# A two-layer transformer in one kernel: other work between a layer's end and the first products of the next

## The chip, the cores and the metric

The kernel runs on one core of one Trainium2 chip. The metric is the device time of one execution in microseconds (us). The kernel before was timed three times; the median is 2736.37 us.

## What is computed

512 tokens of 2048 features go through two layers of a hybrid attention block and then a third block (a pooling mixer, a state-space mixer and a gated embedding). In float32 throughout. Cut to what matters here:

```python
def rms_norm(x, w, eps=NORM_EPS):
    xf = x * lax.rsqrt(jnp.mean(x * x, axis=-1, keepdims=True) + eps)
    return xf * w

def hybrid_layer(x, ...):
    h = rms_norm(x, pre_w)
    proj = h @ w_in                      # 2048 -> 5952, split into q, k, v, gates, latents c_q, c_kv ...
    qc = rms_norm(c_q, q_norm_w) @ w_uq  # latent of 512
    kvc = rms_norm(c_kv, kv_norm_w) @ w_ukv
    y = ...                              # three kinds of attention, gated
    out = y @ w_out
    return x + rms_norm(out, post_w)     # "new x"
```

The layer runs twice. The second block begins in the same way: norm of x, then `h @ w_in_2`.

## The kernel before

**Layout.** Everything is kept feature-major: a matrix of 512 tokens by 2048 features is 16 tiles of 128 partitions (features) by 512 (tokens), called kt = 0 to 15. A float32 product is made of three matmuls (`product`, lines 1792 to 1794): high part of the weights by high part of the activations, high weights by low activations, low weights by high activations. So for every weight tile ScalarE makes the high part (`w_hi`, line 560) and GpSimd the low one (`w_lo`, line 547), and for every activation tile ScalarE makes `act_hi` and VectorE `act_lo` (line 1006, `lo_part`). Weights come in units of 512 KB through a ring of four slots (unit u lies in slot u mod 4): the DMA queue of SyncE refills a slot when the low part of its unit is made; ScalarE splits a unit into a slot when TensorE is done with the unit four before it (`split_one`).

**What sets the order.** There is no scheduler. Each engine has its own program, written out by hand, and the engines wait for each other by semaphores. ScalarE's program carries the weight splits as calls of `split_until` and `through`, placed between its other work, and all of it runs strictly in that order.

**From one layer to the next.** At the end of layer l, after the last product with `w_out`, all of this follows (it happens twice: the first handoff goes to layer 1, the second to the third block):
- `ones_product` sums squares over the partitions on TensorE, `root` takes the square root on ScalarE, `rms` the reciprocal on VectorE (lines 1864, 588, 1027). The result `rstd` stands in SBUF.
- A loop over the 16 tiles on VectorE: tile times `rstd` (line 1425), times the weight and plus the old x (line 1426, the old x stands in `wide`), then the low part of the tile before (line 1006), and one addition to the running sum of squares (line 1435).
- The same loop on ScalarE: high part (line 782), square (line 784); after tiles 7, 11 and 15 some weight units are split, after tiles 7 and 15 half of x is stored to DRAM (line 788, semaphore `x_out`).
- TensorE runs `first_pairs`: for each tile kt four output tiles (two in `gemm_ps`, two in `s_ps`), 12 matmuls, each tile after its low part is there. In front of each group of four tiles it waits for the two weight units of the group.

**Behind it.** TensorE goes on with `ckr` (in layer 1 four units of 12 matmuls; after two of them `ones_product` of the new x), then `ckv`, whose results go to `gemm_ps` again, so VectorE must have taken the first results out of it (line 998, `take`). VectorE takes them times `rstd` of the new x, into tiles 12 to 15, and only after the stores of x have landed, because they read those tiles. Then it sums their squares (`square_sum`), for a `ones_product` that comes after three of the four `ckv` units of 24 matmuls.

The very first products, of the input x, go through `first_pairs` as well, with tiles split by `split_x0` (line 689) and `lo_part`.

## Time and profile before

| | |
|---|---|
| median of three runs | 2736.37 us (2735.83 to 2737.54) |
| the profiled execution | 2740.65 us, span of its profile 2738.9 us |
| TensorE matmul | busy 2653.3 us (97% of the span), 12650 matmuls |
| VectorE | 1455.6 us (53%) |
| GpSimd | 1181.3 us (43%) |
| ScalarE | 939.1 us (34%) |
| mean granted TensorE clock | 0.99 |

TensorE leaves some 86 us of the span free, and all other engines are far from full. The table of instructions by line says what each costs; the list of waits says for whom TensorE stood still; the timeline of an engine shows single instructions, with the idle time in front of them and what ended it. A matmul row's length includes its way through the array: in a busy stretch the next one starts well before the row ends.

### The profile page before, as it was taken

What the parts mean: (1) busy time and instruction counts of PE and PEld (TensorE: products, weight loads), DVE (VectorE), ACT (ScalarE), POOL (GpSimd) and SP (SyncE); (2) the same over time, 40 slices, a digit from 0 to 9 for tenths busy, and PEclk for the clock granted to TensorE, in tenths of its full rate; (3) what the DMA queues carried; (4) which work ended last, traced back from release to release, by engine and by line L of the source; (5) the groups of instructions that cost most, each with busy time, mean ns of one, the idle gap of its engine ahead of it and who ended that gap; (6) DMA issues with size and microseconds to landing.
All of it is one profiled execution on the core that took longest, in us unless ns stands there. A gap on an engine that the chain in (4) does not pass through costs nothing. (4 is left out here: it accounts for less than half of the span.)

```text
span 2738.9 us, 34832 instructions
## 1 busy us (share of the span) xinstructions
PE 2653.3 (97%) x12650; PEld 2110.3 (77%) x12650; DVE 1455.6 (53%) x1962; ACT 939.1 (34%) x1898; POOL 1181.3 (43%) x860
## 2 busy tenths in 40 slices
PE   8999999999999899999999999989999999999997
PEld 6877877877788678787777778868777688788885
DVE  6453137449622835312654973286799996300524
ACT  5233214225422423321431552241455443322321
POOL 6542443442354345244344234535333356455552
PEclk9999999999999999999999999999999999999998
DMA  5332332221433243233223143224322233433332
GB/s 180 101 112 63 100 85 69 77 85 47 161 92 100 78 130 115 70 92 92 62 77 88 51 149 105 93 106 137 96 78 85 93 123 108 155 96 96 106 93 77
DMA packets 246202, 268.74 MB, mean 98 GB/s; under 512 B 20544, under 2 KB 237248, under 8 KB 243648
## 3 DMA queue, kind: packets, MB, share of 16 engines
q1 hardware_dynamic: 240512, 222.33, 27.4%
q10 hardware_dynamic: 5568, 44.74, 4.1%
q8 instruction: 82, 1.34, 0.2%
q14 instruction: 40, 0.33, 0.0%
HBM read 246.06 MB, written 20.97 MB: 97 GB/s over the span
## 5 line engine op out<-in xcount | busy, mean ns | idle before, releaser
L547 POOL TENSOR_TENSOR w_lo<-w_raw,w_hi 128x512 fp32r<-128x512 f32 x856 | 1181.1, 1403 | 1516.2 <-ACT w_hi L560 1516.0
L1792 PE MATMUL gemm_ps<-act_hi,w_hi 128*128 128x512 f32 x2720 | 1086.0, 399 | 48.2 <-DVE act_lo L1006 36.9
L1794 PE MATMUL gemm_ps<-act_hi,w_lo 128*128 128x512 f32 x2720 | 1063.2, 391 | 0.0
L1793 PE MATMUL gemm_ps<-act_lo,w_hi 128*128 128x512 f32 x2720 | 1062.8, 391 | 0.0
L560 ACT CAST w_hi<-w_raw 128x512 fp32r<-128x512 f32 x856 | 486.5, 618 | 1321.5 <-PE gemm_ps L1794 1105.5
L1792 PEld LDWEIGHTS gemm_ps<-act_hi,w_hi 128*128 128x128 f32 x2720 | 512.5, 188 | 188.3 <-issue 55.3
L1794 PEld LDWEIGHTS gemm_ps<-act_hi,w_lo 128*128 128x128 f32 x2720 | 512.5, 188 | 109.1
L1793 PEld LDWEIGHTS gemm_ps<-act_lo,w_hi 128*128 128x128 f32 x2720 | 513.1, 189 | 105.8 <-issue 4.3
L998 DVE TENSOR_TENSOR tiles<-gemm_ps,rstd 128x512 f32<-128x512 f32 (+1 forms) x50 | 33.9, 689 | 262.3 <-PE gemm_ps L1794 258.5
L1405 DVE COPY tiles<-gemm_ps 128x512 f32 x28 | 19.4, 692 | 179.0 <-PE gemm_ps L1794 178.6
L1737 DVE TENSOR_TENSOR tiles<-gemm_ps,att 128x512 f32<-128x512 f32 x16 | 11.0, 690 | 141.6 <-PE gemm_ps L1794 141.6
L1792 PE MATMUL to_ps<-act_hi,w_hi 128*128 128x512 f32 x192 | 75.9, 395 | 0.0
L1072 DVE TENSOR_TENSOR att<-to_ps,sin_t 128x512 f32<-128x512 f32 x40 | 27.5, 689 | 88.9 <-PE to_ps L1893 88.8
L1794 PE MATMUL to_ps<-act_hi,w_lo 128*128 128x512 f32 x192 | 74.7, 389 | 0.0
L1793 PE MATMUL to_ps<-act_lo,w_hi 128*128 128x512 f32 x192 | 74.7, 389 | 0.0
L1110 DVE TENSOR_REDUCE small<-s_ps 128x1 f32<-128x128 f32 (+5 forms) x48 | 26.7, 557 | 81.4 <-PE s_ps L1937 81.0
L1952 PE MATMUL to_ps<-cst,att 128*128 128x128 f32 x384 | 59.1, 278 | 7.0 <-ACT att L638 4.6
L616 ACT ACTIVATE att<-att,small 128x256 f32<-128x256 f32 (+1 forms) x128 | 60.1, 473 | 15.1 <-DVE small L1106 14.2
L1952 PEld LDWEIGHTS to_ps<-cst,att 128*128 128x128 f32 x384 | 47.7, 142 | 18.4 <-issue 5.5
L1767 DVE SCALAR_TENSOR_TENSOR att<-att 128x512 f32 x14 | 11.3, 807 | 90.0 <-ACT att L971 90.0
L1083 DVE TENSOR_TENSOR tiles<-tiles,att 128x512 f32<-128x512 f32 x36 | 56.1, 1560 | 1.2
L623 ACT ACTIVATE att<-s_ps,small 128x128 f32<-128x128 f32 (+1 forms) x64 | 31.8, 500 | 71.0 <-DVE small L1111 71.0
(396 smaller groups left out, 3158.1 us busy)
## 6 DMA issues: line engine op xcount, KB each, us to landing
w_raw<-in_w_in_dram SPq DMA_DIRECT2D x248, 512.0 KB
w_raw<-in_w_out_dram SPq DMA_DIRECT2D x96, 512.0 KB
w_raw<-in_w_ple_gate_dram SPq DMA_DIRECT2D x32, 512.0 KB
gate_scratch<-att ACTq DMA_DIRECT2D x16, 512.0 KB, 2.7
x_scratch<-tiles ACTq DMA_DIRECT2D x4, 2048.0 KB, 8.4
att<-x_scratch ACTq DMA_DIRECT2D x2, 4096.0 KB, 12.6
w_raw<-in_w_glu_dram SPq DMA_DIRECT2D x32, 256.0 KB
tiles<-in_x_dram ACTq DMA_DIRECT2D x4, 1024.0 KB, 8.0
```

Of the source, the lines that this page charges most:

```text
L547: ins = pool.tensor_tensor(w_lo[:, s, k], w_raw[:, s, k], w_hi[:, s, k].bitcast(F32), ALU.subtract)
L560: act.copy(w_hi[:, slot, k:k + 2], w_raw[:, slot, k:k + 2]).then_inc(whi_done, 1)
L616: act.activation(v, v, ACT.Exp, bias=sm[:, 4 + j:5 + j], scale=SCALE[br], accum_out=sm[:, 8 + j:9 + j])
L623: last = act.activation(prob[n % 3][:, c * 512:c * 512 + nk], src, ACT.Exp, bias=sm[:, 4 + c:5 + c], scale=SCALE[br], accum_out=sm[:, 8 + ...
L998: tt(dst, ps[:, f, :], scale[:], ALU.mult).then_inc(bank_taken[f], 1)
L1072: tt(sq[:, n % 2], t_ps[:, n % 2, :], sin_t[:], ALU.mult).then_inc(rope_read, 1)
L1083: tt(t, t, sq[:, n % 2], ALU.add).then_inc(roped, 1)
L1110: own.link(dve.reduce_max(sm[:, 0:nc_], src, AX))
L1792: pe.matmul(ps, left_hi, right_hi, start=first, stop=False, skip_group_check=True)
L1793: pe.matmul(ps, left_hi, right_lo, start=False, stop=False, skip_group_check=True)
L1794: return pe.matmul(ps, left_lo, right_hi, start=False, stop=last, skip_group_check=True)
L1952: mm = pe.transpose(t_ps[:, a, k * 128:(k + 1) * 128], prob[n % 3][:, a * 512 + k * 128:a * 512 + (k + 1) * 128], ident)
```

## The change

- The reciprocal of the handoff is written to PSUM (`o_ps[:, 0]`), and tile times reciprocal to `o_ps[:, 1]`; both were in SBUF. Before each such product VectorE now waits until the multiply-add of the tile before is done with `o_ps[:, 1]`.
- Of the 15 additions of squares in the loop, 6 stay; the rest is done after the loop in wider additions, and tiles 14 and 15 go to a second input of `ones_product` (one more matmul, at layer 1 and the third block).
- `first_pairs` waits for the high part of a tile, does the eight matmuls with it, then waits for the low part and does the other four.
- The results of the first products are copied out by ScalarE as they are, to tiles 4 to 7 (`raw_out`), and VectorE multiplies them by `rstd` there later (`scale_raw`).
- x is stored in three parts (tiles 0 to 7, 8 to 11, 12 to 15), with a semaphore each.

The core of the diff (left out: the semaphores of the store, the same waits in the third block):

```diff
@@ -670,6 +671,13 @@
 
+            def raw_out(key, first, pairs_out):
+
+                for r in range(pairs_out):
+                    for f in range(2):
+                        act.wait_ge(mm_done, unit_end(key, 6 + r) + f + 1)
+                        act.copy(tiles[:, first + 2 * r + f], (gemm_ps, s_ps)[r][:, f, :]).then_inc(bank_taken[f], 1)
+
             n_par = 0
@@ -707,6 +715,7 @@
             through(("cq", 0), 8)
+            raw_out(("cq", 0), 4, 2)
 
@@ -715,7 +724,7 @@
                         act.wait_ge(mm_done, unit_end(("ukv", l - 1), 4))
-                    act.copy(sub_hi[:, kt], tiles[:, 12 + kt]).then_inc(lat_hi, 1)
+                    act.copy(sub_hi[:, kt], tiles[:, 4 + kt]).then_inc(lat_hi, 1)
                 through(("uq", l), 4)
@@ -783,13 +793,18 @@
                     if kt % 4 == 3 and kt > 4:
-                        split_until(at[("cq", 1) if l == 0 else ("si", 0)][0] + {7: 6, 11: 8, 15: 12 if l else 14}[kt])
-                    if kt % 8 == 7:
-                        act.dma_start(x_dram[:, kt - 7:kt + 1, :], tiles[:, kt - 7:kt + 1, :]).then_inc(x_out, 16)
+                        split_until(at[("cq", 1) if l == 0 else ("si", 0)][0] + {7: 6, 11: 8, 15: 12}[kt])
+                    if kt in (7, 11, 15):
+                        part = slice(0 if kt == 7 else kt - 3, kt + 1)
+                        act.dma_start(x_dram[:, part, :], tiles[:, part, :]).then_inc(x_out[kt // 4 - 1], 16)
                 if l == LAYERS - 1:
-                    act.wait_ge(sq_sum, 15 * l + 13)
+                    act.wait_ge(sq_sum, 6 * l + 6)
                     act.dma_start(att[:, SSM_AT:SSM_AT + SSM_COLS],
                                   ssm_params[:, POLE_COLS:POLE_COLS + SSM_COLS]).then_inc(ssm_in, 16)
+                if l == 0:
+                    act.wait_ge(x_out[0], 16)
+                    raw_out(("cq", 1), 4, 2)
+                    split_until(at[("cq", 1)][0] + 14)
                 root(f"x{l + 1}")
@@ -1020,12 +1035,18 @@
 
-            def rms(norm):
+            def rms(norm, dst=None):
 
                 to = rstd_lat if norm[0] == "c" else rstd[:]
                 dve.wait_ge(sqrt_done, NORMS[norm] + 1)
-                dve.reciprocal(to, to).then_inc(rstd_done, 1)
+                dve.reciprocal(to if dst is None else dst, to).then_inc(rstd_done, 1)
                 dve.wait_ge(rstd_done, NORMS[norm] + 1)
+
+            def scale_raw(first, count):
+
+                for k in range(first, first + count):
+                    mark = own.mark(tt(tiles[:, k], tiles[:, k], rstd[:], ALU.mult))
+                own.wait(mark)
 
@@ -1266,14 +1287,12 @@
                     rms(f"x{l}")
-                    dve.wait_ge(x_out, 32 * l)
-                for r in range(2):
-                    for f in range(2):
-                        round_done(("cq", l), 6 + r, f)
-                        take(f, tiles[:, 12 + 2 * r + f], ps=s_ps if r else gemm_ps)
-                dve.wait_ge(bank_taken[0], at[("cq", l)][1] + 3)
-                dve.wait_ge(bank_taken[1], at[("cq", l)][1] + 3)
-                square_sum(12)
+                    for s in x_out[:2]:
+                        dve.wait_ge(s, 16 * l)
+                for b in bank_taken:
+                    dve.wait_ge(b, at[("cq", l)][1] + 3)
+                scale_raw(4, 4)
+                square_sum(4)
                 dve.nop().then_inc(bank_taken[0], 1)
@@ -1283,12 +1302,14 @@
                         rms(f"cq{l}")
-                        latent(l, 0, 12, "qn")
+                        latent(l, 0, 4, "qn")
                         dve.wait_ge(rcol_tp, l + 1)
                         dve.tensor_copy(C("rcol", 0, 4), t_ps[:, 0, :].rearrange("p (t n) -> p t n", t=4)[:, :, 0])\
                             .then_inc(rcol_done, 1)
 
                 dve.wait_ge(lat_ready, 8 * l + 4)
+                if l:
+                    dve.wait_ge(x_out[2], 16 * l)
                 for r, (u, dst) in enumerate(((0, 12), (1, 14), (None, 9))):
@@ -1415,25 +1436,32 @@
                     dve.tensor_copy(tiles[:, 14 + f], gemm_ps[:, f, :]).then_inc(bank_taken[f], 1)
-                rms(f"post{l}")
+                rms(f"post{l}", o_ps[:, 0, :])
                 dve.wait_ge(x_back, 16 * (l + 1))
                 pre = [C("pre", 16 + kt) if l == 0 else C("gain2", kt) for kt in range(KT)]
                 for kt in range(KT + 2):
                     if kt < KT:
                         if kt >= 14:
                             dve.wait_ge(bank_taken[kt % 2], at[("wo", l)][1] + 9)
-                        own.link(tt(tiles[:, kt], tiles[:, kt], rstd[:], ALU.mult))
-                        stt(tiles[:, kt], tiles[:, kt], C("post", 16 * l + kt), wide[:, kt],
+                        if kt:
+                            dve.wait_ge(xnew, KT * l + kt)
+                        own.link(tt(o_ps[:, 1, :], tiles[:, kt], o_ps[:, 0, :], ALU.mult))
+                        stt(tiles[:, kt], o_ps[:, 1, :], C("post", 16 * l + kt), wide[:, kt],
                             ALU.mult, ALU.add).then_inc(xnew, 1)
                     if 1 <= kt <= KT:
                         dve.wait_ge(xnew, KT * l + kt)
                         lo_part(f"x{l + 1}", kt - 1, pre[kt - 1])
-                    if kt > 2:
+                    if 10 <= kt < 16:
                         dve.wait_ge(sq_done, KT * (l + 1) + kt - 1)
-                        if kt > 3:
-                            dve.wait_ge(sq_sum, 15 * l + kt - 3)
-                        tt(wide[:, 0], wide[:, 0], wide[:, kt - 2], ALU.add).then_inc(sq_sum, 1)
-                dve.wait_ge(sq_sum, 15 * (l + 1))
+                        if kt > 10:
+                            dve.wait_ge(sq_sum, 6 * l + kt - 10)
+                        tt(wide[:, 7], wide[:, 7], wide[:, kt - 2], ALU.add).then_inc(sq_sum, 1)
+                dve.wait_ge(sq_sum, 6 * (l + 1))
+                own.link(tt(wide_flat[:, 0:4 * T], wide_flat[:, 0:4 * T], wide_flat[:, 4 * T:8 * T], ALU.add))
+                own.link(tt(wide_flat[:, 0:2 * T], wide_flat[:, 0:2 * T], wide_flat[:, 2 * T:4 * T], ALU.add))
+                own.mark(tt(wide[:, 0], wide[:, 0], wide[:, 1], ALU.add))
+                dve.wait_ge(sq_done, KT * (l + 2))
+                own.link(tt(wide[:, 14], wide[:, 14], wide[:, 15], ALU.add))
                 dve.nop().then_inc(ssq_in, 1)
@@ -1856,10 +1886,10 @@
 
-            def ones_product(norm, squares=(sq[:, 0],), lasts=0):
+            def ones_product(norm, squares=(sq[:, 0],), lasts=None):
                 pe.wait_ge(ssq_in, SSQ[norm])
                 for i, s in enumerate(squares):
-                    if i:
+                    if i and lasts is not None:
                         pe.wait_ge(last_sq, lasts + i)
@@ -1872,16 +1902,21 @@
                         pe.wait_ge(bank_taken[1], r0 + 1)
+                    groups = [(p, f, slice(128 * f, 128 * f + 128)) for p in range(2) for f in range(2)]
                     for k in range(UK):
-                        ready_tiles(version, 4 * j + k + 1)
-                        for p, ps in enumerate((gemm_ps, s_ps)):
-                            slot = (2 * j + p) % RING
-                            for f in range(2):
-                                w = slice(128 * f, 128 * f + 128)
-                                mm = product(ps[:, f, :], w_hi[:, slot, k, w], w_lo[:, slot, k, w], act_hi[:, 4 * j + k],
-                                             act_lo[:, 4 * j + k], j == 0 and k == 0, j == 3 and k == 3)
-                                if k == UK - 1:
-                                    mm.then_inc(mm_done, 1)
+                        first, last, kt = j == 0 and k == 0, j == 3 and k == 3, 4 * j + k
+                        pe.wait_ge(hi_done, VERS[version] + kt + 1)
+                        for p, f, w in groups:
+                            ps, slot = (gemm_ps, s_ps)[p][:, f, :], (2 * j + p) % RING
+                            pe.matmul(ps, w_hi[:, slot, k, w], act_hi[:, kt], start=first, stop=False, skip_group_check=True)
+                            pe.matmul(ps, w_lo[:, slot, k, w], act_hi[:, kt], start=False, stop=False, skip_group_check=True)
+                        ready_tiles(version, kt + 1)
+                        for p, f, w in groups:
+                            ps, slot = (gemm_ps, s_ps)[p][:, f, :], (2 * j + p) % RING
+                            mm = pe.matmul(ps, w_hi[:, slot, k, w], act_lo[:, kt], start=False, stop=last,
+                                           skip_group_check=True)
+                            if k == UK - 1:
+                                mm.then_inc(mm_done, 1)
 
@@ -2008,7 +2043,7 @@
                     if j == 1:
-                        ones_product(f"x{l}", [wide[:, 0]])
+                        ones_product(f"x{l}", [wide[:, 0], wide[:, 14]] if l else [wide[:, 0]])
                 u0, first_free = at[("ckv", l)][0], at[("cq", l)][1] + 1
```

Three places in the engines' order. First VectorE in the first handoff, around tiles 4 to 6 (`tiles` is x, `col` the norm weights, `att` the old x or the squares, `to_ps` holds `o_ps`). Before:

```order
L1425 TENSOR_TENSOR tiles<-tiles,rstd 128x512
L1426 SCALAR_TENSOR_TENSOR tiles<-tiles,col,att 128x512 [waits dve_own]
L1006 SCALAR_TENSOR_TENSOR act_lo<-tiles,col,act_hi 128x512 [waits hi_done,xnew]
L1435 TENSOR_TENSOR att<-att 128x512 [waits sq_sum,sq_done]
L1425 TENSOR_TENSOR tiles<-tiles,rstd 128x512
```

and changed:

```order
L1448 TENSOR_TENSOR to_ps<-tiles,to_ps 128x512 [waits xnew]
L1449 SCALAR_TENSOR_TENSOR tiles<-to_ps,col,att 128x512 [waits dve_own]
L1021 SCALAR_TENSOR_TENSOR act_lo<-tiles,col,act_hi 128x512 [waits hi_done,xnew]
L1448 TENSOR_TENSOR to_ps<-tiles,to_ps 128x512 [waits xnew]
L1449 SCALAR_TENSOR_TENSOR tiles<-to_ps,col,att 128x512 [waits dve_own]
```

The addition is gone from these tiles, and the product has a wait of its own.

Then VectorE behind the last tile of that handoff, changed:

```order
L1021 SCALAR_TENSOR_TENSOR act_lo<-tiles,col,act_hi 128x512 [waits hi_done,xnew]
L1460 TENSOR_TENSOR att<-att 128x2048 [waits sq_sum]
L1461 TENSOR_TENSOR att<-att 128x1024 [waits dve_own]
L1462 TENSOR_TENSOR att<-att 128x512 [waits dve_own]
L1464 TENSOR_TENSOR att<-att 128x512 [waits sq_done]
L1042 RECIPROCAL rstd<-rstd 128x512 [waits dve_own,sqrt_done]
L1048 TENSOR_TENSOR tiles<-tiles,rstd 128x512 [waits bank0_taken,x_out1,bank1_taken,x_out0,rstd_done]
```

Four wider additions stand behind the last low part where two of 512 stood, and the first read of the new `rstd` no longer reads a bank that TensorE waits for.

Last ScalarE behind tile 15 of the first handoff, changed (the casts are splits of weight units):

```order
L561 CAST w_hi<-w_raw 128x512 [waits mm_done,raw_in3]
L561 CAST w_hi<-w_raw 128x512
L799 DMA x_scratch<-tiles 128x2048
L679 COPY tiles<-gemm_ps 128x512 [waits mm_done,x_out0]
L679 COPY tiles<-gemm_ps 128x512 [waits mm_done]
L679 COPY tiles<-s_ps 128x512 [waits mm_done] x2
L561 CAST w_hi<-w_raw 128x512 [waits mm_done,raw_in0]
```

Before, four more casts stood ahead of the store, and no copy; now the store comes first, then the copies, then those four casts, and only then the root.

## Rows read from the trace of the kernel before

**Rows 1.** TensorE's waits in the whole span: us in total, times, longest

```profile
PE gemm_ps L1792 <- DVE act_lo L1006: 36.9, 13, 12.8
```

**Rows 2.** Timelines at the start: first matmul, first low part, second weight unit

```profile
12.77 0.76 PE L1792 MATMUL gemm_ps<-act_hi,w_hi 128*128 128x512 f32 x1 [12.77 <-DVE act_lo L1006]
...
10.76 1.87 DVE L1006 SCALAR_TENSOR_TENSOR act_lo<-tiles,col,act_hi 128x512 fp32r<-128x512 f32 x1 [9.42 <-ACT act_hi L689]
...
10.81 1.27 POOL L547 TENSOR_TENSOR w_lo<-w_raw,w_hi 128x512 fp32r<-128x512 f32 x1
```

**Rows 3.** Timelines of the first handoff: first high part on ScalarE, then TensorE

```profile
897.77 0.72 ACT L782 ACTIVATE act_hi<-tiles,col 128x512 fp32r<-128x512 f32 x1 [4.93 <-DVE tiles L1426]
...
899.93 0.76 PE L1792 MATMUL gemm_ps<-act_hi,w_hi 128*128 128x512 f32 x1 [7.82 <-DVE act_lo L1006]
905.91 0.39 PE L1794 MATMUL gemm_ps<-act_hi,w_lo 128*128 128x512 f32 x1
908.22 0.39 PE L1792 MATMUL gemm_ps<-act_hi,w_hi 128*128 128x512 f32 x1
910.94 0.39 PE L1792 MATMUL gemm_ps<-act_hi,w_hi 128*128 128x512 f32 x1
```

**Rows 4.** TensorE, first handoff: both later waits, the first fast matmul after them

```profile
934.19 0.50 PE L1792 MATMUL gemm_ps<-act_hi,w_hi 128*128 128x512 f32 x1 [1.33 <-DVE act_lo L1006]
939.12 0.47 PE L1792 MATMUL gemm_ps<-act_hi,w_hi 128*128 128x512 f32 x1 [1.92 <-DVE act_lo L1006]
943.30 0.39 PE L1794 MATMUL s_ps<-act_hi,w_lo 128*128 128x512 f32 x1
```

**Rows 5.** TensorE, second handoff: start, first fast matmul, three waits

```profile
1793.39 0.76 PE L1792 MATMUL gemm_ps<-act_hi,w_hi 128*128 128x512 f32 x1 [7.82 <-DVE act_lo L1006]
1796.81 0.39 PE L1794 MATMUL s_ps<-act_hi,w_lo 128*128 128x512 f32 x1
1817.71 0.47 PE L1792 MATMUL gemm_ps<-act_hi,w_hi 128*128 128x512 f32 x1 [0.78 <-DVE act_lo L1006]
1827.65 0.50 PE L1792 MATMUL gemm_ps<-act_hi,w_hi 128*128 128x512 f32 x1 [1.50 <-DVE act_lo L1006]
1832.59 0.47 PE L1792 MATMUL gemm_ps<-act_hi,w_hi 128*128 128x512 f32 x1 [1.92 <-DVE act_lo L1006]
```

**Rows 6.** GpSimd in its first burst of weight splits in the first handoff

```profile
915.71 6.39 POOL L547 TENSOR_TENSOR w_lo<-w_raw,w_hi 128x512 fp32r<-128x512 f32 x4 [24.07 <-ACT w_hi L560]
```

**Rows 7.** VectorE lines over the span: duration ns min/median/max, first and last start

```profile
L998 DVE TENSOR_TENSOR tiles<-gemm_ps,rstd x50: 678/692/693, 71.3 to 2182.1; 128x512 f32<-128x512 f32 x34, 128x512 f32 x16
...
L1425 DVE TENSOR_TENSOR tiles<-tiles,rstd x32: 681/684/1780, 896.3 to 1835.6; 128x512 f32<-128x512 f32 x32
...
L1541 DVE TENSOR_TENSOR to_ps<-to_ps,sin_t x8: 699/700/700, 1947.9 to 2170.0; 128x512 f32<-128x512 f32 x8
```

**Rows 8.** TensorE where ckv starts, layers 0 and 1, and VectorE in layer 1

```profile
72.17 0.47 PE L1792 MATMUL gemm_ps<-act_hi,w_hi 128*128 128x512 f32 x1 [1.26 <-DVE tiles L998]
...
967.06 0.65 PE L1792 MATMUL gemm_ps<-act_hi,w_hi 128*128 128x512 f32 x1 [3.41 <-POOL w_lo L547]
970.78 0.40 PE L1792 MATMUL gemm_ps<-act_hi,w_hi 128*128 128x512 f32 x1
...
966.22 1.29 DVE L998 TENSOR_TENSOR tiles<-gemm_ps,rstd 128x512 f32<-128x512 f32 x2 [3.59 <-DMA x_scratch<-tiles]
```

**Rows 9.** TensorE around the ones product of the new x, layer 1

```profile
957.17 1.02 PE L1864 MATMUL to_ps<-att,ones 128*128 128x512 f32 x2
...
958.73 0.39 PE L1792 MATMUL to_ps<-act_hi,w_hi 128*128 128x512 f32 x1
```

**Rows 10.** Wide additions on VectorE at the start, and GpSimd beside them

```profile
33.41 4.41 DVE L1181 TENSOR_TENSOR att<-att 128x4096 f32<-128x4096 f32 x1
37.86 7.20 DVE L1181 TENSOR_TENSOR att<-att 128x2048 f32<-128x2048 f32 x3
...
36.81 9.39 POOL L547 TENSOR_TENSOR w_lo<-w_raw,w_hi 128x512 fp32r<-128x512 f32 x4 [4.53 <-ACT w_hi L560]
```

14 lines of the change are left out of this document (9 added, 5 removed).

## The prediction

> **What bounds the kernel now.** I read the page first: TensorE is busy 97% of the span, every other engine at most 53%. So the time moves only where TensorE stands still, runs at the lower clock, or gets more to do. The list of its waits names the places [rows 1]: 36.9 us, 13 times, for a low part of an activation. The timelines split this sum: 12.77 us at the start [rows 2], 7.82 us at the beginning of each handoff [rows 3, 5], and five short waits inside the handoffs [rows 4, 5]; the rest is outside the change. Two more waits stand behind `first_pairs`, where `ckv` needs an output bank: 1.26 us in layer 0 and 3.41 us in layer 1 [rows 8]. The second is put down to GpSimd, but VectorE's row beside it shows the cause: it had waited 3.59 us for the store of x, and took the bank at 966.22.
>
> In full flow a tile of `first_pairs` (12 matmuls) takes TensorE 910.94 - 908.22 = 2.72 us, 0.227 us a matmul [rows 3]. Right after a handoff's gap the pitch is 0.43 us, the engine at 1.2 instead of 2.4 GHz. A wait costs its idle time and some 0.16 us more, since a row of 0.39 us overlaps the next in full flow.
>
> **The change, part by part** (gains in us).
>
> *Start, 0.5.* The first matmul waits for the first low part, which took 1.87 us (10.76 to 12.63) beside GpSimd. With high parts first it waits for the second weight unit only, done at 10.81 + 1.27 = 12.08 [rows 2]. With the 0.14 us between release and first matmul that is 12.2 instead of 12.77. Bounds: 0 and 0.6.
>
> *First matmul of each handoff, 1.2 each, 2.4 in all.* The first high part ends at 897.77 + 0.72 = 898.49, so TensorE could start at 898.6 instead of 899.93 [rows 3]: 1.3. I take off 0.1 for the detour through PSUM. The low part is needed only eight slow matmuls (3.4 us) later; before, it was there 1.3 us after the high part.
>
> *VectorE's loop.* Before it has four instructions a tile, 2.65 us, as long as TensorE's 2.72; each time GpSimd splits four half units (6.39 us [rows 6]) VectorE's rows go from 0.68 to 1.78 us [rows 7], and it falls behind. Now tiles 0 to 9 have three instructions, some 2.15 us; tiles 10 to 15 four. Two of them have one operand in PSUM. Rows with such an operand never got longer, not even beside GpSimd: 678 to 693 ns in all 50 [rows 7]; only the low part and the addition can still be held up. The product both reads and writes PSUM; its nearest row, of just this form, takes 700 ns against 684 in SBUF [rows 7]. The new wait for the multiply-add costs a semaphore, 0.06 us; queued behind it are that product and the low part, and for them TensorE waits. Worked through tile by tile, the low part of tile 15 is made 8 us before TensorE ends, so none of the five waits remains:
> - first handoff: 1.33 + 1.92 + 2 x 0.16 = 3.6, and the slow stretch behind the second, 939.12 to 943.30, 11 pitches in 4.18 instead of 2.50 us, 1.7 [rows 4]. Together 5.2.
> - second handoff: 0.78 + 1.50 + 1.92 + 3 x 0.16 = 4.7 [rows 5].
>
> *The clock at a handoff's start, 0.* Fourteen slow pitches (899.93 to 905.91) in the first, eight (1793.39 to 1796.81) in the second, after the same idle 7.82 us [rows 3, 5]. The idle time becomes 6.5 us. I leave both as they are; the bounds are the two swapped for each other (1.2 us each way), and no slow stretch at all (2.8 + 1.6 = 4.4 gained).
>
> *The bank of ckv.* ScalarE copies the first two results at once, so TensorE finds its banks free. Layer 0: 1.26 + 0.16 = 1.4. There the copies stand behind the root of x, some 2 us before they are needed, and no store is in the way. Layer 1: 3.41 + 0.16, and nine slow pitches behind it (967.06 to 970.78, 3.72 instead of 2.04) 1.7, in all 5.3 [rows 8]. Behind the end of `first_pairs` ScalarE has two units to split and the four copies, at most 8 x 0.72 = 5.8 us by its row of the same size [rows 3]; queued behind are two weight units, the root and two more units. The first of these units, whose low part takes GpSimd 2 x 1.6 us [rows 6], is ready at about 5.8 + 0.7 + 3.2 = 9.7 us, and needed at 12.6 (4 x 2.72 of `ckr` and two ones matmuls). This is the thinnest cover, 3 us.
>
> *scale_raw.* Four products in SBUF take the place of four takes from PSUM, so GpSimd can stretch them to 1.78 us: up to 4.4 us later for the sum of squares of the latent. That sum is needed three `ckv` units (16.3 us) after `ckv` starts, and is there about 6 us earlier. Nothing.
>
> *The late sums.* Behind the last low part come 2048, 1024, 512 and 512 elements. By the row of 4096 in 4.41 us they take 4.9 us. The three instructions beside GpSimd took 7.20 us for 3584 elements instead of 3.9 [rows 10], 1.1 us more for each instruction and not a multiple of its length: 4.9 + 4 x 1.1 = 9.3 at the most. From the last low part (8 us before the end of `first_pairs`) this ends at most 1.3 us behind that end; `ones_product` asks for it 5.4 us behind it. So hidden. GpSimd is held up in turn (9.39 us for four instead of 6.39 [rows 10, 6]), 3 to 5 us, just when `ckr`'s units are split; this uses up cover of the paragraph before last. The Trainium skill, SBUF — State Buffer, section Who interferes with whom, calls this an exclusive lock: whoever comes second stands until the other instruction is over. By that rule the delay is one per instruction, as the row shows; were it a factor, as in 1.78 / 0.68, the sums would take 12.7 us, and `ones_product` would still just find them.
>
> *One more ones matmul*, at two places, on TensorE's path: from 957.17 to 958.73 stand one of them and three matmuls, 1.56 - 0.68 = 0.88 [rows 9]. Minus 1.8 for both.
>
> *Store in three parts.* One DMA issue more (0.3 us of ScalarE's queue) at each handoff, hidden; in layer 1 nobody who holds up TensorE waits for the last part.
>
> Sum: 0.5 + 2.4 + 5.2 + 4.7 + 1.4 + 5.3 - 1.8 = 17.7 us. The profiled execution took 2740.65 us, and would take 2723.0. It lies 4.3 us above the median of the runs, 2736.37; against that the forecast is **2718.7 us**. Everything behind the third block's start moves ahead as a whole, as its chain hangs on TensorE.
>
> The Trainium skill, Perfetto Trace Analysis, section Optimizing Scalar/DVE Operations, speaks against the change: it states an access overhead of about 60 ns for VectorE on SBUF and 125 on PSUM. By it each tile would need 0.1 to 0.2 us more and the sum would be 17.4; the 16 ns of rows 7 decide here.
>
> **The rivals.**
> 1. *ScalarE or the sums come late.* The copies, the splits and the wide additions fall into the same 10 us as GpSimd's densest stretch; TensorE then waits for `w_lo` in `ckr` or at `ckv`, or for the sum at `ones_product`. For it: thin covers of 3 us, estimated from rows of another order. Against it: all covers are positive. Price: 2 to 5 us at each handoff; in all some 7, a gain of 10.7: 2725.7. Chance 0.17.
> 2. *The weights bind inside the handoff.* The pair of units for tiles 12 to 15 is split only after ScalarE's tile 11, and GpSimd needs about 6 us for it (6.39 [rows 6]). If TensorE comes early it stands for GpSimd instead of for the low part. I expect 1.5 to 4 us of cover. Without it the 5.2 + 4.7 are lost: gain 7.8, 2728.6. Chance 0.05.
> 3. *The clock.* The gap is shorter and no short waits follow. If neither handoff starts slowly, 4.4 more: 2714.3. Against it: after 1.92 us of idleness the clock fell once [rows 4] and once not [rows 5], so 6.5 is hardly short enough. The Trainium skill, TensorE: Matmul & The Clock Gate, Part 1, says the number of slow matmuls changes from run to run, as the 14 and 8 here do. Chance 0.08.
> 4. *Slower.* The single bank for the product chains product, multiply-add and next product. If each of the three hand-overs costs 0.5 us more than in SBUF, a tile takes 2.15 + 1.5 = 3.65 us on VectorE, more than TensorE's 2.72, and TensorE waits at every tile: `first_pairs` 4 + 15 x 3.65 = 58.8 us, instead of 51.5 and 49.8 now (16 x 2.72, the slow start of 2.8 or 1.6, the waits' 5.2 or 4.7). That is 16.3 lost, 2.4 + 0.5 + 1.4 + 5.3 - 1.8 gained: 8.5 slower, 2744.9. It turns into a loss from about 3.4 us a tile. No row shows such a hand-over cost. Chance 0.04.
> 5. *The change doesn't do what it says*: the copies at layer 0 stand behind the root, at layer 1 behind splits, so the banks are no earlier. Then 6.7 is lost: 2725.4. The order of ScalarE's rows speaks against it. Chance 0.03.
>
> **The numbers.** The forecast has 0.63. About 0.2%, 5.5 us, is what a measurement of this kernel can tell from no change. Rivals 1, 2, 3 and 5 are faster by more than that; with a little taken off for small gains of rivals 1 and 2: faster 0.92, same 0.04, slower 0.04. The range reaches from rival 3 with part of the clock's other bound, 2713.5, to rival 1 at the worse end of its price, 2727.0; outside lie rivals 2 and 4.
>
> **What would show it.** Right: VectorE's loop rows at 0.70 and 0.75 us with only low parts and additions stretched; no wait inside `first_pairs`, which takes about 46 us; `ckv` behind `ckr` without a gap; two rows more of ones matmuls. Wrong: TensorE waiting for `w_lo` or for high parts, `ones_product` waiting for VectorE, or slow stretches in other places.

## The result, and the profile after

| | before | after |
|---|---|---|
| median of the runs | 2736.89 us (2735.83 to 2737.54, 4 runs) | 2719.26 us (2717.07 to 2719.49, 4 runs) |
| ratio | 1 | 0.9932, 95% interval 0.9919 to 0.9944 |
| profiled execution, span | 2740.65, 2738.9 us | 2719.48, 2717.7 us |
| granted TensorE clock, mean | 0.990 | 0.993 |

17.6 us less by the medians, where 17.7 were forecast. The two spans differ by 21.2 us; the sections behind the experiments show where the rest lies.

The page of the kernel after, engines: busy time, share of the span, instructions.

```profile
PE 2646.2 (97%) x12654; PEld 2106.0 (77%) x12654; DVE 1463.4 (54%) x1952; ACT 941.8 (35%) x1906; POOL 1189.7 (44%) x860
```

TensorE's waits after, the lines that answer to [rows 1] (us in total, times, longest):

```profile
PE gemm_ps L1911 <- ACT act_hi L792: 13.1, 2, 6.5
PE gemm_ps L1911 <- POOL w_lo L548: 12.1, 1, 12.1
...
PE gemm_ps L1822 <- DVE act_lo L1021: 0.6, 3, 0.2
```

Of 36.9 us of waits for a low part 0.6 are left. The start now waits for the weights and the two handoffs for the first high part. No wait inside `first_pairs` is in the list.

TensorE's timeline after (start, duration, engine, line, operation, tiles, shapes, count, idle time before and what ended it), to be held against [rows 2, 3, 5, 8, 9]:

```profile
12.13 0.79 PE L1911 MATMUL gemm_ps<-act_hi,w_hi 128*128 128x512 f32 x1 [12.13 <-POOL w_lo L548]
...
894.38 0.77 PE L1911 MATMUL gemm_ps<-act_hi,w_hi 128*128 128x512 f32 x1 [6.54 <-ACT act_hi L792]
...
939.98 0.39 PE L1822 MATMUL to_ps<-act_hi,w_hi 128*128 128x512 f32 x1
...
945.43 1.88 PE L1894 MATMUL to_ps<-att,ones 128*128 128x512 f32 x4
946.75 0.79 PE L1822 MATMUL to_ps<-act_hi,w_hi 128*128 128x512 f32 x1
...
952.63 0.39 PE L1822 MATMUL gemm_ps<-act_hi,w_hi 128*128 128x512 f32 x1
...
1776.25 0.77 PE L1911 MATMUL gemm_ps<-act_hi,w_hi 128*128 128x512 f32 x1 [6.54 <-ACT act_hi L792]
```

`first_pairs` of the first handoff took 51.8 us before (899.93 to 951.72) and takes 45.6 (894.38 to 939.98). At 952.63 `ckv` follows `ckr` with no gap, where 3.41 us stood before.

VectorE's lines in the loop of the handoff (ns min/median/max; 1448 the product, 1449 the multiply-add, 1021 the low part), beside [rows 7]:

```profile
L1448 DVE TENSOR_TENSOR to_ps<-tiles,to_ps x32: 681/689/697, 892.0 to 1811.4; 128x512 f32<-128x512 f32 x32
L1449 DVE SCALAR_TENSOR_TENSOR tiles<-to_ps,col,att x32: 751/751/753, 892.7 to 1812.2; 128x512 f32<-128x512 f32 x32
L1021 DVE SCALAR_TENSOR_TENSOR act_lo<-tiles,col,act_hi x48: 736/744/1865, 10.8 to 1814.1; 128x512 fp32r<-128x512 f32 x48
```

The product's longest row went from 1780 to 697 ns; only the low part and the additions that stayed in the loop (685 ns, longest 1780) are still stretched. Behind the loop, VectorE's wide additions and ScalarE's new order:

```profile
932.89 2.28 DVE L1460 TENSOR_TENSOR att<-att 128x2048 f32<-128x2048 f32 x1
935.21 2.20 DVE L1461 TENSOR_TENSOR att<-att 128x1024 f32<-128x1024 f32 x1
937.44 1.66 DVE L1462 TENSOR_TENSOR att<-att 128x512 f32<-128x512 f32 x1
939.03 1.77 DVE L1464 TENSOR_TENSOR att<-att 128x512 f32<-128x512 f32 x1
```

```profile
940.56 0.33 ACTq L799 DMA_DIRECT2D x_scratch<-tiles  x1
940.83 1.14 ACT L561 CAST w_hi<-w_raw 128x512 fp32r<-128x512 f32 x2
941.87 1.06 ACT L679 COPY tiles<-gemm_ps 128x512 f32<-128x512 f32 x2
942.83 1.08 ACT L679 COPY tiles<-s_ps 128x512 f32<-128x512 f32 x2
943.78 1.17 ACT L561 CAST w_hi<-w_raw 128x512 fp32r<-128x512 f32 x2
947.34 1.14 ACT L561 CAST w_hi<-w_raw 128x512 fp32r<-128x512 f32 x2 [2.39 <-DMA w_raw<-in_w_in_dram]
...
948.49 0.67 ACT L589 ACTIVATE rstd<-to_ps,col 128x512 f32<-128x512 f32 x1
```

The sums are ready at 940.8 us and asked for at 945.43. The last part of x is on its way at 940.56, where the kernel before issued its last half at 957.46. (The two traces are 11.7 us apart by then.) The root of x's norm at 948.49 stands behind a split that waited 2.39 us for the load of a weight unit; this line matters below.

In layer 1 the sum of squares for the latent's norm now comes just in time. Its last addition, and the ones matmul that reads the sum:

```profile
966.34 1.66 DVE L1032 TENSOR_TENSOR att<-att 128x512 f32<-128x512 f32 x1
...
968.96 1.02 PE L1894 MATMUL to_ps<-att,ones 128*128 128x512 f32 x2
```

### The profile page after: what moved, and what is told of

Read it like the earlier page. It is cut to its first block and busy times, and to the rows that moved or that the text cites. A ratio compares the mean times of both kernels' runs of the same rounds, so it can differ in the third digit from the quotient of the medians.

```text
span 2717.7 us, 34829 instructions
## 1 busy us (share of the span) xinstructions
PE 2646.2 (97%) x12654; PEld 2106.0 (77%) x12654; DVE 1463.4 (54%) x1952; ACT 941.8 (35%) x1906; POOL 1189.7 (44%) x860
## 5 line engine op out<-in xcount | busy, mean ns | idle before, releaser
L1824 PE MATMUL gemm_ps<-act_hi,w_lo 128*128 128x512 f32 x2624 | 1023.3, 390 | 0.0
L1823 PE MATMUL gemm_ps<-act_lo,w_hi 128*128 128x512 f32 x2624 | 1022.9, 390 | 0.0
L1822 PEld LDWEIGHTS gemm_ps<-act_hi,w_hi 128*128 128x128 f32 x2624 | 492.9, 188 | 139.0 <-issue 32.0
L1824 PEld LDWEIGHTS gemm_ps<-act_hi,w_lo 128*128 128x128 f32 x2624 | 493.0, 188 | 104.4
L1823 PEld LDWEIGHTS gemm_ps<-act_lo,w_hi 128*128 128x128 f32 x2624 | 493.4, 188 | 102.2 <-issue 4.3
```

The costliest lines, as they stand in the source:

```text
L1822: pe.matmul(ps, left_hi, right_hi, start=first, stop=False, skip_group_check=True)
L1823: pe.matmul(ps, left_hi, right_lo, start=False, stop=False, skip_group_check=True)
L1824: return pe.matmul(ps, left_lo, right_hi, start=False, stop=last, skip_group_check=True)
```

## The experiments

Eleven variants and the changed kernel once more. Runs of one job share the chip and the runs of the kernel before.

| run | what differs from the kernel after | median us (range, runs) | ratio to before, 95% |
|---|---|---|---|
| job 1, before 2737.39 | | | |
| e1_takes_47 | VectorE takes, into tiles 4 to 7; no raw copies | 2722.72 (2719.27 to 2723.75, 4) | 0.9946 (0.9929 to 0.9963) |
| e2_takes_1215 | the same into tiles 12 to 15, behind all stores | 2721.77 (2720.33 to 2722.33, 4) | 0.9941 (0.9924 to 0.9957) |
| e3_low_with_high | old order in `first_pairs` | 2724.02 (2723.39 to 2724.69, 4) | 0.9949 (0.9932 to 0.9965) |
| e4_loop_sums | all sums in the loop, one ones matmul | 2722.11 (2721.73 to 2723.53, 4) | 0.9944 (0.9927 to 0.9961) |
| job 2, before 2739.13 | | | |
| c_after | nothing | 2718.71 (2718.04 to 2719.99, 5) | 0.9926 (0.9912 to 0.9939) |
| e7_fold | one addition more, one ones matmul less | 2718.83 (2717.93 to 2719.80, 5) | 0.9926 (0.9913 to 0.9940) |
| e9_split_first | as e2, splits ahead of the last store | 2719.17 (2718.88 to 2721.30, 4) | 0.9929 (0.9914 to 0.9945) |
| e10_both | as e9, and the store in two parts | 2726.00 (2725.61 to 2730.10, 4) | 0.9951 (0.9936 to 0.9967) |
| job 3, before 2736.65 | | | |
| e8_two_part | as e2, store in two parts | 2726.70 (2724.66 to 2727.65, 5) | 0.9961 (0.9947 to 0.9975) |
| e5_sbuf_norm | norm back in SBUF | 2728.26 (2727.59 to 2730.05, 7) | 0.9968 (0.9957 to 0.9980) |
| e6_sbuf_loop_sums | norm in SBUF, sums in the loop | 2729.09 (2726.77 to 2730.23, 7) | 0.9965 (0.9954 to 0.9977) |
| job 4, before 2739.88 | | | |
| e11_raw_two_part | store in two parts, the rest as after | 2721.70 (2719.45 to 2722.98, 5) | 0.9931 (0.9918 to 0.9945) |

### What the raw copies are worth

e1 puts VectorE's four takes back, into the tiles that the raw copies use (so only the first two stores are waited for):

```diff
-            raw_out(("cq", 0), 4, 2)
-                    act.wait_ge(x_out[0], 16)
-                    raw_out(("cq", 1), 4, 2)
-                scale_raw(4, 4)
+                for r in range(2):
+                    for f in range(2):
+                        round_done(("cq", l), 6 + r, f)
+                        take(f, tiles[:, 4 + 2 * r + f], ps=s_ps if r else gemm_ps)
```

> The changed kernel, but VectorE takes the first products out times rstd as before (into tiles 4 to 7, waiting for the first two parts of the store), and ScalarE copies nothing. Theory A, the copies free the bank: all of the 6.6 us that the trace shows where ckv starts (1.4 in layer 0, 5.2 in layer 1) is lost again, 2725.9. Theory B, most of it came from the store and from the order of ScalarE's program: in the changed kernel rstd stands at 952.55 us and ckv starts at 952.63, so with takes TensorE waits some 1.4 us in layer 0 and 0.9 in layer 1, and the time is 2721.6.

e2 does the same with tiles 12 to 15 and waits for all three stores:

> As the kernel before in this place: VectorE takes the first products times rstd into tiles 12 to 15 and waits for all three parts of the store. Theory B: the last part is issued at 940.6 us instead of 957.5 and should land before rstd is there (952.6), so the same 2721.6 as with tiles 4 to 7, and no idle row of VectorE that ends by the store. Theory A: 2725.9, with VectorE waiting for the store some 3.5 us as before.

Both medians lie nearer to theory B (2721.6) than to A (2725.9). TensorE in e2 at the start of `ckv` in layer 0 and in layer 1, and VectorE's take in layer 1:

```profile
70.99 0.47 PE L1822 MATMUL gemm_ps<-act_hi,w_hi 128*128 128x512 f32 x1 [1.27 <-DVE tiles L1010]
...
954.41 0.47 PE L1822 MATMUL gemm_ps<-act_hi,w_hi 128*128 128x512 f32 x1 [0.21 <-DVE tiles L1010]
...
953.57 1.29 DVE L1010 TENSOR_TENSOR tiles<-gemm_ps,rstd 128x512 f32<-128x512 f32 x2
```

In layer 0 the old wait of 1.26 us is back. In layer 1 it is 0.21 us instead of 3.41, though VectorE takes the banks as before: the take no longer waits for a store. So by the traces the copies are worth 1.4 us in layer 0 and 0.3 to 0.5 in layer 1, and the 5.3 us of the forecast's step come from elsewhere. By the medians e1 costs 3.5 and e2 2.5 us; what lies beyond 1.8 us is no more than single runs of one kernel differ by.

### The store's place and its size

What else changed there is ScalarE's order (last store ahead of the splits up to unit 14) and the store's parts. Three runs on e2 take these apart. e9 restores the order, e8 the two parts, e10 both:

```diff
-                        split_until(at[("cq", 1) if l == 0 else ("si", 0)][0] + {7: 6, 11: 8, 15: 12}[kt])
+                        split_until(at[("cq", 1) if l == 0 else ("si", 0)][0] + {7: 6, 11: 8, 15: 12 if l else 14}[kt])
-                    if kt in (7, 11, 15):
-                        part = slice(0 if kt == 7 else kt - 3, kt + 1)
+                    if kt in (7, 15):
+                        part = slice(kt - 7, kt + 1)
```

> The variant with VectorE's takes into tiles 12 to 15 (it ran at 2721.8 us), with ScalarE's splits up to unit 14 put ahead of the last store of x again, as the kernel before had them; the store stays in three parts. There the last store would be issued at about 949 us instead of 941.7 and, at the 5.4 us of a 1 MB store in the trace after, land at 954.4 us; the take behind it began at 953.6. Theory (the part of the gain at the start of ckv in layer 1 came from when the store lands, and either its earlier place or its halved size is nearly enough): 1.0 us more, 2722.8 us, and the take waits about 0.9 us for the store. Rival (the place in ScalarE's program is what paid, whatever the size): the 5 us of that step come back, 2726.5 us. Second rival (the store never mattered in this variant): 2721.8 us.

> The variant with takes into tiles 12 to 15 (2721.8 us), with the store of x in two parts of 2 MB again, but in its early place, ahead of the splits. It is issued at 941.7 us and, at the 8.7 us that such a store took in the kernel before, lands at 950.4 us, 3 us ahead of the take at 953.6. Theory: nothing changes, 2721.8 us, within 1 us, no wait for the store. Rival (the size alone makes the wait): the take waits, 2724 to 2726 us.

> As the run with the splits first, and the store of x in two parts of 2 MB again, both as in the kernel before (where such a store took 8.7 us). The second part is issued at about 949 us and lands at 957.7 us, against a take that could begin at 953.6. Theory (size and place add up, and only together they cost much): the take waits 4.1 us for the store, and the kernel takes 4 to 4.5 us more than the variant with takes into tiles 12 to 15, 2726.0 us. Rival (the size does not matter, the place alone does): the same time as the run with the splits first. Second rival: no wait and 2721.8 us.

e9: VectorE's take and the store ahead of it:

```profile
946.62 0.33 ACTq L798 DMA_DIRECT2D x_scratch<-tiles  x1
...
952.89 1.29 DVE L1008 TENSOR_TENSOR tiles<-gemm_ps,rstd 128x512 f32<-128x512 f32 x2 [0.57 <-DMA x_scratch<-tiles]
```

The wait for the store is there, 0.57 us, and costs nothing that the runs show: 2719.17 us, 0.5 over the changed kernel in the same job (2718.71) and under all three numbers of the expectation. With the store in three parts, its place in ScalarE's order is worth nothing that shows.

e10: the take waits 4.46 us for the 2 MB store, TensorE 4.05 us for the take, and 14 matmuls at the low clock follow (959.45 to 965.56). 2726.0 us, as expected, and the same path as in the kernel before:

```profile
958.61 1.29 DVE L1008 TENSOR_TENSOR tiles<-gemm_ps,rstd 128x512 f32<-128x512 f32 x2 [4.46 <-DMA x_scratch<-tiles]
...
959.45 0.77 PE L1820 MATMUL gemm_ps<-act_hi,w_hi 128*128 128x512 f32 x1 [4.05 <-DVE tiles L1008]
```

e8 is the surprise: the big store in its early place costs as much, 2726.7 us, and nobody waits for it. ScalarE, VectorE and TensorE in e8:

```profile
942.77 0.33 ACTq L798 DMA_DIRECT2D x_scratch<-tiles  x1
...
952.54 1.14 ACT L561 CAST w_hi<-w_raw 128x512 fp32r<-128x512 f32 x2 [5.95 <-DMA w_raw<-in_w_in_dram]
...
953.69 0.67 ACT L589 ACTIVATE rstd<-to_ps,col 128x512 f32<-128x512 f32 x1
...
954.39 3.35 DVE L1039 RECIPROCAL rstd<-rstd 128x512 f32<-128x512 f32 x1 [11.58 <-ACT rstd L589]
...
958.62 0.47 PE L1822 MATMUL gemm_ps<-act_hi,w_hi 128*128 128x512 f32 x1 [3.34 <-DVE tiles L1010]
```

The store runs beside the load of a weight unit, and the split that needs this unit waits 5.95 us (2.54 in e2 with its 1 MB store). The load is slower and not issued later: from its issue to its last byte it takes 8.4 us (944.12 to 952.52), in e2 5.1 us (943.19 to 948.31). The root of x's norm stands behind that split in ScalarE's program, so against TensorE root, reciprocal and take are each some 3 us later than in e2; TensorE waits 3.34 us and then runs 8 matmuls at the low clock (959.61 to 962.98; the expectation of e11 below says 10). My expectation, that size and place cost only together, fell; the rival's number, 2724 to 2726, was nearly right, by a way that neither named. So the number of e10 was hit, but the small store is what pays, in either place.

e11 then undoes only the three parts and keeps the copies:

> The changed kernel with one thing undone: x is stored in two parts of 2 MB again; ScalarE's raw copies, its order, the late sums, the norm in PSUM and the high parts first stay. With VectorE's takes in place of the raw copies the 2 MB store cost 5 to 7 us: beside it the load of a weight unit came 3.4 us later (ScalarE idle 5.95 us for it instead of 2.5), the root of x's norm stood behind that split in ScalarE's program, the reciprocal came at 954.4 us instead of 950.2, the take behind it, and TensorE waited 3.3 us and then ran 10 matmuls at the low clock. Here the banks are released by ScalarE's copies at 942 to 944 us, ahead of root and reciprocal. Theory (the copies and the store in parts stand in for each other at the start of ckv in layer 1): the root is as late as there, at about 953.7 us, but TensorE passes into ckv without a wait for a bank; at most a wait for the low part of the late weight unit of about 1 us; 2719.5 us, between 2718.5 and 2721.5. Rival (the late weight unit itself holds TensorE, whoever empties the banks): a wait of 2 to 4 us for w_lo near 955 us and the slow matmuls behind it, 2723 to 2726 us.

```profile
950.24 1.14 ACT L561 CAST w_hi<-w_raw 128x512 fp32r<-128x512 f32 x2 [5.34 <-DMA w_raw<-in_w_in_dram]
...
951.39 0.67 ACT L589 ACTIVATE rstd<-to_ps,col 128x512 f32<-128x512 f32 x1
...
969.69 1.12 PE L1894 MATMUL to_ps<-att,ones 128*128 128x512 f32 x2 [0.64 <-DVE att L1032]
```

The weight unit is late again (5.34 us), the root with it, but TensorE enters `ckv` without a wait: ScalarE had emptied the banks at 944 us. Only the sum for the latent's norm comes 0.64 us late. The median, 2721.7 us, is 0.2 above the top of what the theory gave and well under the rival's 2723 to 2726; the profile shows the theory's mechanism. So copies and small parts stand in for each other at this place. Without the copies two parts cost 5 to 7 us by the medians (e8 against e2, e10 against e9) and the same by the traces at this place (4.7 and 6.9). With the copies they cost 3.0 us by the medians, but only 0.9 at this place; in the trace the rest lies behind it, near 1590, 1780 and 2150 us, where the clock stays low longer than in the trace after. That the store causes this rest is not shown.

### High parts first

e3 puts the matmuls of `first_pairs` back into the old order, three for each weight tile behind both parts of the activation:

```diff
-                        pe.wait_ge(hi_done, VERS[version] + kt + 1)
...
+                        ready_tiles(version, 4 * j + k + 1)
...
+                                mm = product(ps[:, f, :], w_hi[:, slot, k, w], w_lo[:, slot, k, w], act_hi[:, 4 * j + k],
+                                             act_lo[:, 4 * j + k], j == 0 and k == 0, j == 3 and k == 3)
```

> The changed kernel with the old order inside first_pairs (each tile waits for its low part). Theory: only the start of each first_pairs is later, by 0.6 us at the kernel's start and 1.3 us in each handoff, 3.2 us in all, 2722.5; no wait inside, since VectorE is ahead. Rival, high parts first is what took the inner waits away: five waits come back, some 10 us, 2732.

```profile
896.22 0.77 PE L1822 MATMUL gemm_ps<-act_hi,w_hi 128*128 128x512 f32 x1 [7.96 <-DVE act_lo L1021]
...
1780.69 0.77 PE L1822 MATMUL gemm_ps<-act_hi,w_hi 128*128 128x512 f32 x1 [7.96 <-DVE act_lo L1021]
```

7.96 us instead of 6.54 at each handoff, 0.41 at the start, and no wait inside. 2724.02 us is 1.5 above the expectation; against the trace after, each handoff loses another 0.9 to 1.3 us behind its first matmul, where the stretch at the low clock is longer (14 and 13 matmuls instead of 10 and 7). I have not separated that from the spread of this stretch between runs.

### Sums late, norm in PSUM

e4 has all 15 additions in the loop and one ones matmul, as before the change:

```diff
-                    if 10 <= kt < 16:
+                    if kt > 2:
-                        tt(wide[:, 7], wide[:, 7], wide[:, kt - 2], ALU.add).then_inc(sq_sum, 1)
+                        tt(wide[:, 0], wide[:, 0], wide[:, kt - 2], ALU.add).then_inc(sq_sum, 1)
```

> The changed kernel with all 15 additions of squares in the loop as before, and one ones matmul. Theory: with the product in PSUM VectorE keeps ahead even with four instructions a tile; the two ones matmuls are saved (1.8 us), at most 1 us is lost for a weight unit in the second handoff: 2717.5 to 2718.5. Rival, the late sums are needed: the waits for the low parts of tiles 11 and 12 come back, 3 to 5 us a handoff, 2724 to 2728.

```profile
924.91 5.94 POOL L548 TENSOR_TENSOR w_lo<-w_raw,w_hi 128x512 fp32r<-128x512 f32 x4 [7.06 <-ACT w_hi L561]
...
930.90 0.50 PE L1906 MATMUL gemm_ps<-act_hi,w_hi 128*128 128x512 f32 x1 [0.53 <-POOL w_lo L548]
...
1813.79 0.50 PE L1906 MATMUL gemm_ps<-act_hi,w_hi 128*128 128x512 f32 x1 [1.58 <-POOL w_lo L548]
```

Missed: 2722.11 us instead of 2717.5 to 2718.5. No low part of x is waited for, but the low part of the *weights* for tiles 12 to 15: with 0.6 us more per tile on VectorE, ScalarE reaches the split behind tile 11 later, and GpSimd's burst begins at 924.91 instead of 919.90 us (1.1 us of this stood already at the start of the handoff). The two waits cost 0.8 and 1.9 us in the trace; another 0.7 us goes in a longer slow stretch at the start of the first handoff, and 0.7 behind the ones matmul of the latent's norm in layer 1, which waits 0.39 us for its sum. The low parts of the weights are the mechanism of my second rival, one edit away from the kernel after.

e5 takes the norm back into SBUF and keeps the rest:

```diff
-                rms(f"post{l}", o_ps[:, 0, :])
+                rms(f"post{l}")
-                        own.link(tt(o_ps[:, 1, :], tiles[:, kt], o_ps[:, 0, :], ALU.mult))
-                        stt(tiles[:, kt], o_ps[:, 1, :], C("post", 16 * l + kt), wide[:, kt],
+                        own.link(tt(tiles[:, kt], tiles[:, kt], rstd[:], ALU.mult))
+                        stt(tiles[:, kt], tiles[:, kt], C("post", 16 * l + kt), wide[:, kt],
```

> The changed kernel with the norm of the new x back in SBUF: the reciprocal goes to rstd and the product to the tile itself, so both operations of a tile read and write SBUF alone, as in the kernel before. Late sums and high parts first stay. Theory (what the norm in PSUM gives is that neither VectorE nor GpSimd waits for the other while weights are split; counted through with the durations of the traces, the last low part comes 3 to 4 us later, which the high parts first and the slow stretch still cover, and GpSimd's next burst of splits starts later too): no wait for a low part, a wait of 0.8 to 2 us for the low part of the weights of the unit behind first_pairs in each handoff, 2.4 to 4.8 us more in all, 2722.7 us, between 2720.5 and 2724.5. Rival (the norm's place is worth nothing once the sums are late): 2719.3 us. Second rival (it carries the whole gain inside the handoffs): 2728 us or more, with waits for act_lo as before.

TensorE where `ckr` starts in both handoffs, then the clock behind the first of them (columns: window, length, busy time and count of PE, PEld, DVE, ACT, POOL, granted clock, DMA share, GB/s):

```profile
942.86 0.53 PE L1820 MATMUL to_ps<-act_hi,w_hi 128*128 128x512 f32 x1 [2.41 <-POOL w_lo L548]
...
1829.43 0.50 PE L1820 MATMUL to_ps<-act_hi,w_hi 128*128 128x512 f32 x1 [2.00 <-POOL w_lo L548]
```

```profile
942.80:946.70 3.90, 3.84 (x10) 3.03 (x11) 2.24 (x2) 1.41 (x3) 3.90 (x4) 0.56 0.84 273
946.70:950.00 3.30, 3.30 (x16) 2.73 (x15) 0.00 (x0) 1.14 (x2) 3.30 (x4) 1.00 0.59 162
```

The waits are where the theory put them, and of its size (4.4 us together, 2.4 to 4.8 expected), but the time is 2728.26 us, 4 above the top of its range. What was left out is the clock: behind each wait TensorE runs 8 matmuls at 1.2 GHz (943.2 to 946.6 and 1830.7 to 1834.1 us), nearly as much lost again. In the trace the first handoff costs 4.3 us in all and the second 3.9. The second rival's 2728 us is hit by the number, not by its waits for `act_lo`. This is the dearest single edit: 9 to 9.5 us by the medians.

e6 undoes both (the two diffs together):

> Both undone at once: norm in SBUF, all 15 sums in the loop and one matmul of ones, with high parts first, raw copies and the store as in the changed kernel. Theory (the edits stand in for each other, and only with both gone do the waits come back): waits for a low part of x of up to 1.5 us and for low parts of weights of 1.7 and 0.7 us in each handoff, 3 to 4 us more in each than the changed kernel's, 1.8 us less for the ones matmuls: 2724.5 us, between 2723 and 2727. Rival (weights alone bind, and the norm's place adds nothing to what the run with the sums in the loop showed): 2722.1 us. Second rival (with VectorE's old work per tile the high parts first alone cannot hold it): 2729 us or more.

```profile
932.47 0.74 PE L1909 MATMUL gemm_ps<-act_lo,w_hi 128*128 128x512 f32 x2 [1.06 <-DVE act_lo L1021]
...
935.28 0.51 PE L1904 MATMUL gemm_ps<-act_hi,w_hi 128*128 128x512 f32 x1 [1.60 <-POOL w_lo L548]
...
947.29 0.50 PE L1815 MATMUL to_ps<-act_hi,w_hi 128*128 128x512 f32 x1 [0.60 <-POOL w_lo L548]
```

Waits for both kinds of low part are back in the sizes named (1.06, 1.60, 0.60), yet 2729.09 us lies 2 above the theory's range and on the second rival's number, again by slow matmuls behind the waits of the second handoff (1.57 and 1.62 us; slow from 1820.57 to 1824). Beside e5 the sums' place no longer shows: once one edit lets a wait in, the other has little left to cost.

### One ones matmul less

```diff
                 own.link(tt(wide[:, 14], wide[:, 14], wide[:, 15], ALU.add))
+                own.link(tt(wide[:, 0], wide[:, 0], wide[:, 14], ALU.add))
-                        ones_product(f"x{l}", [wide[:, 0], wide[:, 14]] if l else [wide[:, 0]])
+                        ones_product(f"x{l}", [wide[:, 0]])
```

> The changed kernel with one addition more in each handoff (the sum of squares 14 and 15 is added to the main sum) and one matmul of ones instead of two. In its profile the sums are ready at 940.8 us and TensorE asks for them at 945.4 us, so one more addition of 0.7 us lies inside the 4.6 us between; a pair of ones matmuls takes 1.88 us where the single one took about 0.9. Theory (the ones matmul lies on TensorE's path with its whole length): 0.88 us less in each handoff, 1.76 in all, 2717.5 us, between 2716.8 and 2718.3. Rival (the time is set behind the matmul, by ScalarE's root, which waits for a weight split until 948.5 us anyway): no change, 2719.3 us.

> The changed kernel unchanged, as the common reference of the runs beside it. Expected 2719.3 us, within 1 us.

```profile
945.70 1.02 PE L1895 MATMUL to_ps<-att,ones 128*128 128x512 f32 x2
946.16 0.80 PE L1823 MATMUL to_ps<-act_hi,w_hi 128*128 128x512 f32 x1
```

From the ones to the next product it takes 0.46 us instead of 1.32 (945.43 to 946.75), so 0.86 us are gone there, as the theory says. The medians, 2718.83 and 2718.71 us, show none of it. Against the trace after, TensorE is 0.59 us ahead at the next product and still 0.57 at 1576 us. What becomes of it behind that can't be told: at the end of attention both wait 2.3 us for ScalarE, and the clock falls behind this wait in e7 (1585.30) and not in the trace after (1585.87), so the two drift by more than what is looked for. So the saving stands at its place and is not shown in the time, and no variant beats the changed kernel.

## Why the prediction was right

The forecast was 2718.7 us, the median is 2719.26. That they agree this closely is partly luck: the steps of the change add up to 19.2 us in the traces where 17.7 were forecast, and against its own runs of the kernel before c_after gains 20.4 us, since the medians of the kernel before lie between 2736.65 and 2739.88 us in the four jobs. Step by step, by how much each matmul comes earlier in the trace after:

| step | forecast | in the trace |
|---|---|---|
| start | 0.5 | 0.44 |
| ckv, layer 0 | 1.4 | 1.42 |
| first matmul of a handoff | 1.2, 1.2 | 1.28, 1.20 |
| inside handoff 1 | 5.2 | 6.19 |
| inside handoff 2 | 4.7 | 5.17 |
| ones matmul | -0.9, -0.9 | -0.86, -0.85 |
| ckv, layer 1 | 5.3 | 5.18 |
| outside the change | 0 | 2.3 near 720 us, -0.3 elsewhere |

- *Start and first matmuls*: as worked out. e3 confirms the order as their cause.
- *VectorE's loop*: "none of the five waits remains" holds, and of the surplus of 1 us in handoff 1 0.7 are the clock, left at 0 in the forecast: ten slow matmuls instead of fourteen. The rest, and the 0.5 us in handoff 2, is some 0.1 us behind each of the five waits beyond its price, and 0.1 from the clock. The reason was incomplete. I argued by low parts of x, but e4 and e5 show that with high parts first it is the weights' low parts that decide (in e6 both bind): VectorE's pace sets when ScalarE gets to the splits, and those when GpSimd starts. The chance of 0.05 for rival 2 was for the kernel as it is, and there it did not come; but its cover is what e4 (0.6 us more a tile) uses up. e5 uses up the cover of rival 1: TensorE waits for the weights' low part in `ckr`.
- *The product in PSUM*: 689 ns against 684, no stretch. In e5, with the product in SBUF, its longest row is 1784 ns again, and the time 9 us more. Rival 4's chain of hand-overs did not come. The Trainium skill, Perfetto Trace Analysis, section Optimizing Scalar/DVE Operations, would put the access at 125 instead of 60 ns; this trace has 5 ns.
- *The late sums*: 9.3 us at the most, and 7.9 in the trace (932.89 to 940.80). Three of the four instructions are 1.0 to 1.1 us over their length (1024 elements 2.20, 512 elements 1.66 and 1.77 us), so the delay is one per instruction. With this the rule of the Trainium skill, SBUF — State Buffer, section Who interferes with whom, agrees.
- *scale_raw*: "Nothing" was right, the cover was not. The sum of the latent was to be there about 6 us early. It ends at 968.00 and is read at 968.96, 1.0 us later: the products take 6.3 us, and four of the seven instructions of the sum are stretched as well (1.66 to 1.78 us). In the kernel before it was ready at 973.86 and read at 985.10. e4 and e11, which start this chain later, wait for the sum (0.39 and 0.64 us).
- *ckv in layer 1*: the size was right, the cause was not. The step said "ScalarE copies the first two results at once, so TensorE finds its banks free" and gave the copies all 5.3 us; of the store in three parts it said "hidden". e2 and e9 reach the same start, to 0.5 us, without copies. It is the smaller store: a 2 MB one makes VectorE wait for it (e10) or delays a weight load and with it root and reciprocal (e8). The copies protect from the second (e11); from the first they should as well, since VectorE's take is gone, but no run has both the late store of 2 MB and the copies. So either edit alone would have given most of this term.
- *The parts don't simply add up.* Undone singly they cost, by the medians, 9 to 9.5 (norm), 4.8 (order), 3.0 (store; 0.9 at its place), 2.9 (sums) and 0.5 to 3.5 us (copies; 1.8 in the traces), against a gain of 17.6 to 20.4 in all. Two undone together show it: norm and sums cost about 10 us (e6), less than the 12 of the two singly; store and copies cost 7 to 8 us (e8), more than the two singly, as either of them suffices.

## What to carry to other kernels

Ask of each instruction in a strictly ordered program what a late *load* ahead of it would hold up: here a bigger store on one queue made a weight unit late, and a norm three engines further on. A short wait of TensorE must be priced with the clock that may fall behind it: waits of 2.0 and 2.4 us cost about 4 each in e5, though a wait of 2.3 us elsewhere left the clock up in 15 of 28 cases. And an edit that frees an engine should be judged by what this engine triggers next (the splits here), not by the wait that it removes.
